# Two mixing layers rebuilt: one Block per layer, one ring of 68 weight slots, the delta rule in 84 steps between k-tiles

## What is computed

```python
def second_block(x, ...):
    for l in range(2):
        h = rms_norm_2(x, norm_w[l])
        p = h @ w_in[l]                       # 2048 x 6668
        qa, ka, va, za, ub, zb, qkv_c, b_c, a_c, zc = _split_cols(p)
        # branch A: 12 query heads of 64, 4 key heads, a causal window of 128, sinks
        oa = sliding_window_sink_attention(qa, ka, va, sinks[l]) * silu(za)
        # branch B: gated unit, 31-tap causal convolution on 512 channels, layer norm, 512 x 512
        ob = conformer_conv_module(ub, ...) * silu(zb)
        # branch C: 6 heads of 128, gated delta rule in chunks of 64 tokens
        oc = gated_deltanet(qkv_c, b_c, a_c, c_conv_w[l], c_a_log[l], c_dt_bias[l])
        oc = rms_norm_2(oc, c_onorm_w[l]) * silu(zc)
        x = x + concatenate([oa, ob, oc]) @ w_out[l]

def gated_delta_rule_chunked(q, k, v, g, beta):
    lower = where(strict, k*beta @ k.T * decay, 0)
    u, w = triangular_solve(lower + eye, [v*beta, k*beta*exp(gc)])
    for each chunk of 64:                     # four chunks
        v_new = u_i - w_i @ S                 # S is 0 before the first chunk
        o_i = (q_i * exp(g_i)) @ S + intra_i @ v_new
        S = S * exp(g_last) + (k_i * exp(g_last - g_i)).T @ v_new
```

## Time and profile before

| | |
|---|---|
| median of 3 runs | 2265.16 us (2264.9 to 2267.46) |
| the profiled execution's own time | 2267.13 us |
| its span | 2264.9 us |
| PE busy | 2066.9 us (91%) |
| DVE busy | 1328.0 us (59%) |
| ACT busy | 1083.8 us (48%) |
| HBM read | 321.78 MB |

### The profile page before, as it was taken

One profiled execution on the slowest core, in us unless ns is written; L12 is line 12 of the kernel. 1 busy time (PEld: TensorE's weight loads), 2 busy tenths in 40 slices (PEclk: granted clock), 3 DMA queues, 4 the chain that ended last, 5 costly groups with the idle time before them and its releaser, 6 DMA issues. The chain is left out here.

```text
span 2264.9 us, 32432 instructions
## 1 busy us (share of the span) xinstructions
PE 2066.9 (91%) x13116; PEld 1858.4 (82%) x13116; DVE 1328.0 (59%) x1900; ACT 1083.8 (48%) x1379; POOL 20.9 (1%) x22
## 2 busy tenths in 40 slices
PE   5999999999999999959798997779799789996979
PEld 5999889998888888859688996778698689985967
DVE  4887745554444465446647675854457375767633
ACT  5777645554333333356633466323456333663132
POOL 0001000000000000000000000000000000000000
PEclk9999999999999999979889898899899798998989
DMA  5455454444555556534244342006443243430043
GB/s 192 168 190 183 172 186 149 150 156 173 190 188 193 191 176 239 186 118 149 75 159 175 109 179 91 1 1 242 149 174 112 96 172 125 171 130 18 1 171 127
DMA packets 52403, 329.94 MB, mean 146 GB/s; under 512 B 7472, under 2 KB 9904, under 8 KB 14384
## 3 DMA queue, kind: packets, MB, share of 16 engines
q1 hardware_dynamic: 52272, 328.09, 40.3%
HBM read 321.78 MB, written 6.29 MB: 145 GB/s over the span
## 5 line engine op out<-in xcount | busy, mean ns | idle before, releaser
L350 DVE TENSOR_TENSOR w_lo<-w_raw,w_hi 128x2048 fp32r<-128x2048 f32 x184 | 425.8, 2315 | 392.4 <-ACT w_hi L343 392.3
L343 ACT ACTIVATE w_hi<-w_raw 128x2048 fp32r<-128x2048 f32 x184 | 352.3, 1918 | 404.6 <-PE z L377 304.9
L222 PE MATMUL z<-xn_hi,w_hi 128*128 128x256 f32 x1600 | 469.5, 293 | 33.8 <-DVEq L177 17.4
L222 PE MATMUL z<-xn_hi,w_lo 128*128 128x256 f32 x1600 | 458.8, 287 | 0.0
L222 PE MATMUL z<-xn_lo,w_hi 128*128 128x256 f32 x1600 | 458.2, 286 | 0.0
L194 DVE TENSOR_TENSOR w_lo<-w_raw,w_hi 128x2048 fp32r<-128x2048 f32 x104 | 238.4, 2292 | 195.6 <-ACT w_hi L190 195.5
L222 PEld LDWEIGHTS z<-xn_hi,w_hi 128*128 128x128 f32 x1600 | 310.0, 194 | 43.2 <-DVEq L177 19.4
L190 ACT ACTIVATE w_hi<-w_raw 128x2048 fp32r<-128x2048 f32 x104 | 199.1, 1914 | 277.6 <-PE z L222 260.8
L222 PEld LDWEIGHTS z<-xn_lo,w_hi 128*128 128x128 f32 x1600 | 310.6, 194 | 4.4 <-issue 4.3
L222 PEld LDWEIGHTS z<-xn_hi,w_lo 128*128 128x128 f32 x1600 | 309.0, 193 | 0.0
L377 PE MATMUL z<-w_hi,xn_hi 128*128 128x512 f32 x576 | 230.1, 399 | 0.0
(11 more groups left out here) (469 smaller groups left out, 3043.0 us busy)
## 6 DMA issues: line engine op xcount, KB each, us to landing
w_raw<-in_w_dram SPq DMA_DIRECT2D x288, 1024.0 KB, 4.8
gate_w<-in_lru_w_dram SPq DMA_DIRECT2D x8, 512.0 KB, 5.6
x_state<-state_dram SPq DMA_DIRECT2D x2, 2048.0 KB, 7.9
x_first<-in_x_dram SPq DMA_DIRECT2D x4, 512.0 KB, 7.7
x_t<-in_x_dram SPq DMA_DIRECT2D x1, 2048.0 KB, 11.7
state_dram<-x_t SPq DMA_DIRECT2D x2, 1024.0 KB, 3.9
din_pw<-in_pw_dram SPq DMA_DIRECT2D x2, 1024.0 KB, 5.5
state_dram<-x_state SPq DMA_DIRECT2D x8, 256.0 KB, 3.9
```

What stands on the lines that cost most here:

```text
L222: ins = pe.matmul(out, a, b, start=first and n == 0, stop=last and n == 2)
L343: act.activation(self.k.w_hi[:, n % SLOTS], self.k.w_raw[:, m % RAW], ACT.Copy).then_inc(self.s.rounded, 1)
L350: dve.tensor_tensor(self.k.w_lo[:, n % SLOTS], self.k.w_raw[:, m % RAW], self.k.w_hi[:, n % SLOTS].bitcast(F32), ALU.subtract).then_inc(se ...
```

## The change

`Stream` and the five phases are gone; `layer_block` is one Block per layer with one `Ring` of 68 slots in a new order: 8 for the gated unit, 2 + 2 for keys and values, 6 queries, 6 `za`, 18 for the heads of branch C (q, k, v in turn), 4 `zb`, 6 `zc`, 16 for `w_out`.

- The attention of unit `h` runs during the three slots of head `h`. Of the four 128 x 128 blocks of a head's scores, the one that the mask fills wholly (first queries, last keys) is no longer computed: scores, mask, softmax, transposes and the mix work on 384 columns and not 512.
- The transposes of the layer's input move from the end of the phase before to the first slot of the layer, two between k-tiles, as the first block has it at its own start.
- The narrow product is turned: the 12 columns are the weights, the tokens move (48 matmuls of 256 columns, line `narrow`), with a transpose behind it.
- Of the four taps of branch C's convolution ACT does the last (a copy with a scale), DVE three.
- The delta rule is cut into 28 batches x 3 groups = 84 steps, PE issuing one between two k-tiles in 14 of the 16 k-tiles of each of the six `zc` slots; DVE and ACT empty them in the same order (`evacuate`) behind the rounding and residual of that slot. The mask of a level is applied when its product leaves PSUM, so `BT` and its multiplication are gone. For the first chunk the products with the empty state are left out, and the copy takes the place of the multiply-add; after the last chunk no state is computed.
- In the last stage ACT takes the root of each group by itself: Ln, Exp, Ln, Exp, Ln, Exp.
- The layer's input is loaded in the middle of the ring, when slot 51 is done.

The diff, without the five phases and `Stream`, which are removed whole; its pieces are, in order, the ring, SP's loads, ACT's roots, two pieces of DVE's program, and PE's (the sum over branch B, one stage of a level, the `zc` slots, the token slots):

```diff
+    with phase(nc, f"layer{layer}", LAYER_SEMS) as s:
+        ring = Ring(k, s, SLOTS_1 + layer * SLOTS_2, SLOTS, SLOTS_2 + (SLOTS if more else 0))
...
+                for n in range(8, SLOTS_2 + 2 * SLOTS):
+                    ring.load(sp, n)
+                    if n == SLOT_OUT2 + 3:
+                        sp.wait_ge(s.used, SLOT_OUT2)
+                        sp.dma_start(x_t[:], t["state"]).then_inc(s.xin, 16)
...
+                ring.round(act, SLOT_OUT2 + 4)
+                for gr in groups:
+                    act.wait_ge(s.osum, gr.n + 1)
+                    act.activation(gr.XT, bank4(gr.b0), ACT.Ln, bias=k.eps[:], scale=1.0 / C_DIM).then_inc(s.orstd, 1)
+                    act.wait_ge(s.orstd, 2 * gr.n + 1)
+                    act.activation(gr.XT, gr.XT, ACT.Exp, scale=-0.5).then_inc(s.orstd, 1)
...
+                    if h == 1:
+                        taps(59, 3)
+                        branch_centre()
...
+                for n in range(SLOT_ZC, SLOT_OUT2):
+                    ring.residual(dve, n + 3)
...
+                    window(n)
...
+                    if n == 29:
+                        pe.wait_ge(s.taps, 2 * 2 * TAPS_B)
+                        pe.wait_ge(s.std, 2)
+                        branch_sum(acc).then_inc(s.bsummed, 1)
...
+                    elif b < 15 and stage == 1:
+                        pe.wait_ge(s.ucopied, 3 * (level - 1) + g + 1)
...
+                        for u in range(4):
+                            ins = pe.matmul(part4(gr.b1, u), gr.XT[:, u], gr.A[:, u], start=True, stop=True)
+                        ins.then_inc(s.xx, 1)
...
+                for n in range(SLOT_ZC, SLOT_OUT2):
+                    first_tick = TICKS * (n - SLOT_ZC)
+                    def between(kk):
+                        if kk < TICKS:
+                            step((first_tick + kk) // G, (first_tick + kk) % G)
+                    pe.wait_ge(s.emptied, n - 9)
+                    ring.features(pe, n, tile(bank_of(n)), k.xn_hi, k.xn_lo, between)
...
+                for c in range(4):
...
+                    for w in range(4):
+                        if c == 0 and w == 1:
+                            for g in range(G):
+                                sum_outputs(g)
+                        if c == 0 and w >= 2:
+                            pe.wait_ge(s.olo, 1 if w == 2 else 3)
+                        ring.tokens(pe, SLOT_OUT2 + 4 * c + w, w, pair(c), k.y_hi, k.y_lo)
```

More of the change, by code:

```diff
@@ L158, in _ @@
                     pe.sem_clear(sem)
[L161 to L218, removed]
-                    w_hi, w_lo = s_hi[:, kk, P * m:P * m + P], s_lo[:, kk, P * m:P * m + P]
-                    pairs = ((w_hi, hi[:, row]), (w_hi, lo[:, row]), (w_lo, hi[:, row]))
-                for n, (a, b) in enumerate(pairs):
-                    ins = pe.matmul(out, a, b, start=first and n == 0, stop=last and n == 2)
-        ins.then_inc(self.s.used, 1)
-    def done(self, i, s):
-        return SLOTS + 4 * i + s + 1
@@ L2433, in out_phase_2 @@
[L2433 to L2458 removed]
+                ring.load(sp, 4)
@@ new lines, in root @@
+                def root(bank, out, sem, before):
+                    act.activation(out, both(bank), ACT.Ln, bias=k.eps[:], scale=1.0 / HEAD_DIM_2).then_inc(sem, 1)
+                    act.wait_ge(sem, before + 1)
+                    act.activation(out, out, ACT.Exp, scale=-0.5).then_inc(sem, 1)
+                ring.round(act, SLOT_KV + 4)
+                key_in(0)
+                ring.round(act, SLOT_KV + 5)
+                key_in(1)
+                ring.round(act, SLOT_KV + 6)
+                act.wait_ge(s.kturned, 2)
@@ L2477, in square @@
+                for gr in groups:
+                    act.wait_ge(s.osteps, 2 * gr.n + 2)
+                    at = 10 + 2 * gr.n
+                    act.activation(k.y_hi[:, at:at + 2], by_head(gr.X), ACT.Copy).then_inc(s.orounded, 1)
+                ring.round(act, SLOT_OUT2 + 5)
+                ring.round(act, SLOT_OUT2 + 6)
                 def square(c):
@@ new lines, in _ @@
+                taps(40, 1)
+                ring.residual(dve, SLOT_ZA + 6)
+                taps(41, 4)
+                glink = chain(dve, s.gchain)
+                dve.wait_ge(s.zturned, 1)
+                for b in range(2):
+                    glink(lambda: dve.tensor_tensor(g_x[:, b], z[3][:, 16 * b + H:16 * b + 2 * H], rows[:, 1], ALU.add))
+                glink(lambda: dve.tensor_scalar(g_0[:], g_x[:], -1.0, None, ALU.mult))
+                glink(lambda: dve.tensor_tensor(g_0[:], g_0[:], g_x[:], ALU.min))
@@ new lines, in _ @@
+                pe.wait_ge(s.opened, 3)
+                for b in range(2):
+                    ring.features(pe, SLOT_KV + b, tile(b), k.xn_hi, k.xn_lo)
+                pe.wait_ge(s.opened, 4)
+                ring.halves(pe, SLOT_KV + 2, 0, (tile(2), tile(3)), k.xn_hi, k.xn_lo)
+                pe.wait_ge(s.turn_in, 16)
+                pe.wait_ge(s.kcopied, 2)
+                pe.wait_ge(s.emptied, 2)
+                pe.matmul(aux[0][:, 0:2 * T], turn[:], q_raw[1][:], start=True, stop=True).then_inc(s.kturned, 1)
```

2135 lines of the change are left out of this document (1011 added, 1124 removed).

## The result

The changed kernel takes **2158.06 us** (median of 4 runs, 2155.96 to 2162.24) against 2266.06 of the kernel before, measured beside it (4 runs, 2264.9 to 2267.46): 0.9525 of it, 95% interval 0.9513 to 0.9537, faster. The forecast was 2157, the range 2075 to 2235. The profiled execution is the slowest of the four, 2162.24 with a span of 2160.5, so its parts add up to 3.5 us more than the forecast's span.

The account below looks back on a forecast made before the run. PE was taken to bound the kernel: 517 us of PE's work and 59 of waits make a layer of 576. Start 986.3 + 576 + seam 14 + 576 + end 4.6 gives 2157 us, range 2075 to 2235.

Parts of the forecast that it names:

- PE's work: PE's own work in one layer at full clock, slots, fp32 inserts and delta steps included: 515 us.
- its price for the masked block: Leaving out a quarter of attention's scores, mixes and transposes was to save PE 4.3 us.
- The head slots: Slots 24 to 41: PE was to wait 20 us in a layer for late DVE and ACT.
- its own 92%: In slots 24 to 41, DVE and ACT each have 117 us of work against PE's 128, in strict order.
- The `zc` slots: Slots 46 to 51, with the delta steps between k-tiles: PE was to wait 17 us in a layer.
- every step pays its round trip: Rival, 5%: PE waits for emptying and two hand-overs at each of 168 delta steps, giving 2323 us.
- The output norm: PE's third token slot waits 12.4 us for `y_lo`, behind slot 56's load, a rounding and the roots.
- 4.8 past the end of slot 52: Slot 56's load, behind the 2 MB of `x_t`, was to land 4.8 us after slot 52 ends.
- The six table loads: In the output norm, ACT loads a table for each Ln and Exp in turn: 7.7 us on PE's wait.
- three waits, 2 each: Clock term: three waits a layer are longer than 3.49 us and cost 2 us each, 6 in all.
- the prediction's own sign of being wrong: The prediction is wrong if the clock is under 0.9 in a `zc` slot without a long wait.
- The end stays: From the last matmul to the kernel's end: 4.6 us, as in the kernel before.

Follow-up runs that it names:

- e3: Changed kernel with PE's sum over branch B behind slot 30 in place of slot 29: 2152.81 us, ratio 0.9505.
- e8: Changed kernel with PE again doing the masked attention block's products and transpose, into columns nobody reads: 2160.29 us, ratio 0.9537.
- e5: Changed kernel with delta steps between k-tiles only where PE had to wait, the others in rows behind slots 50 and 51: 2101.96 us, ratio 0.9276.
- e11: Kernel with e5 and e6 together, one of two copies of flipped scores moved from ACT to DVE: 2088.66 us, against 2087.9 without it.
- e4: Changed kernel with all 84 delta steps in one row behind slot 51, same Block and ring: 2143.91 us, ratio 0.9464.
- e2: Changed kernel with the 2 MB load of x_t issued behind the load of slot 56, not ahead: 2156.74 us, ratio 0.9521.
- e1: Changed kernel with three Ln together, then three Exp, in the output norm, so two table loads for six: 2150.63 us, ratio 0.9497.
- e6: Changed kernel with the roots grouped as in e1 and put ahead of ACT's rounding of slot 56: 2143.3 us, ratio 0.9458.
- e10: Changed kernel with the edits of e5, e6 and e3 together: 2081.88 us, ratio 0.9189.

## Why the prediction was right, and where not

**The sum and its parts.** 576 against 577.7 for the layer is in part luck. The waits came 14 lower and the clock 13 higher. Some 4.7 us of both are one thing on two sides, since a low clock ahead of a wait shortens it by as much (e3: 1.6 + 1.4 + 1.7); that the rest evened out was luck.

**PE's work** held: 515 against 517.4, although its price for the masked block, 4.3, was too low (about 7.5 by e8). For the steps, 130.4 less 34.5 for slots, 12.1 of waits and some 6.8 for the clock leaves 77.0; the forecast was 77, of which 4 were for going to and fro between streamed and fp32 work. e5, which has 15 steps between k-tiles and not 84, needs 73.2, which agrees with that.

**The head slots**: 20 forecast, 12.8 measured. The 5.4 us for DVE's taps came as walked through the queues (5.5), at the place named; the lateness of heads 1 and 2 came as 0.4 and that of heads 4 and 5 as 7.0. What the step did not draw from its own 92% is e3, e8 and e11: PE is not the bound in these slots, and a microsecond taken from a wait or from PE's work is not a microsecond won. The forecast counts leaving out the masked block as 4.3 us won; e8 shows about 0.

**The `zc` slots**: 17 forecast, 12.1 measured, each wait where it was put. Slot 46 has 1.98 and 2.95 (6 forecast), slot 47 has 2.23 (3), the scaled copies 2.40 (4). The rounding and then the residual at each slot's start, about 1 a slot, came as 1.24 in slot 48 and 1.33 in slot 49, some 5 us into the slot, and as nothing in slot 51. DVE's timeline shows the cause:

```profile
1377.82 2.29 DVE L253 TENSOR_TENSOR w_lo<-w_raw,w_hi 128x2048 fp32r<-128x2048 f32 x1 [2.38 <-ACT w_hi L246]
1380.03 0.68 DVE L2037 TENSOR_TENSOR unit<-aux,levels 128x512 f32<-128x512 f32 x1
...
1397.50 2.29 DVE L253 TENSOR_TENSOR w_lo<-w_raw,w_hi 128x2048 fp32r<-128x2048 f32 x1 [2.38 <-ACT w_hi L246]
```

DVE stands for 2.38 us before ACT's rounding, which itself waits for PE's last matmul of the slot before, then takes 2.29 for the residual, and only then empties the next step, on which PE waits until 1380.76. e5 has none of these waits; there the levels stand in a row with no rounding or residual between. The rival that every step pays its round trip is out: in the rows of e4 and e5 the levels run without a wait.

**The output norm**: 12.4 forecast, 9.47 and 8.37 measured. The term "4.8 past the end of slot 52" for the transfer is the one that failed: it cost 1.5 and 0.4 (e2). The rounding has to wait for the end of slot 52 in any case, and that slot began 2.5 us late and ran in part at a clock of 0.50, so that more of the 2 MB passed under it. The six table loads hold (e1, e6). For that order of Ln and Exp, the Trainium skill's ScalarE: Activation LUTs, section on table sets, has one load; the trace after does not agree either, with a load of 1.28 before each of the six. The Trainium skill's ScalarE: Activation LUTs, section What ACT_TABLE_LOAD costs, makes up the about 2.7 us that the prediction names of a load of about 1283 ns and a drain of about 1380 ns. The trace agrees with the load, 1.28, and shows no such drain: a load starts 0.02 us behind the operation before it (1471.60 to 1471.62), and its activation follows at once.

**The clock**: 6 for "three waits, 2 each" was the worst term, 18 measured. In this execution every wait of 1.98 us and more has a stretch at 0.50 with it, nine of them in the layer and not three, each costing 1.7 to 3 beyond the wait. This is also why the forecast's error in the waits did not show: shorter waits than forecast, more of them dear. Slot 46, with no wait over 3, had a mean clock of 0.87, which comes close to the prediction's own sign of being wrong, under 0.9 in a `zc` slot without a long wait.

**Not foreseen**: 2.53 at the first token slot, which needs the bank of slot 51. ACT empties it behind the rounding of slot 55, and both can start only when slot 51 is done.

**Seams**: start 987.1 (986.3 forecast), 13.7 (14, though its four terms add up to 13.3), end 7.3 (4.6). "The end stays" was wrong: the kernel before cleared 3 semaphores on PE there, the changed one clears 26, and PE is at it until 2160.2. The prediction charged more clearing at both starts and not here.

**What was missed altogether**: that the 84 steps between k-tiles are worse than the same steps in a row. The earlier trace rows showed it, sets 0.89 apart without a gap when nothing else was queued on DVE. The prediction used those rows for the price only, and not to ask what the placing itself brings. e4 and DVE's rows above show what that is.

## What to carry over

Put work of a dependent chain between streamed tiles only where the chain to another engine is longer than the rest of its own row; where three groups in rotation already hide it, a row of its own is faster, as the engine that empties it then has nothing else queued. Where two engines hand work to a third in strict order and all are near full, test by adding work to one before taking any away: if the time stays, that engine is not the bound. In an order written by hand, look for the operation that waits for nothing the next one needs (here a rounding ahead of the roots), and move it behind.

## What was not expected of the hardware

- A Block change that clears no semaphores left PE idle for 0.47 us in a running stream; 26 semaphores cleared by PE took 3.0 us.
- In the changed kernel the granted clock fell to 0.50 around or behind each wait of 1.98 us and more in an otherwise full stream, and stayed at 1.00 around waits of 1.24 and 1.33. But the same waits differ between executions: in layer 0 of e3 it stayed at 1.00 around those of 1.98, 2.23, 2.34 and 2.53, in layer 0 of e6 around the one of 2.52 for the root. Behind the wait of 2.20 for `y_lo` it stayed up in e6 and fell in layer 0 of e10. The four executions of the changed kernel stand in the order of their mean clocks, 0.973, 0.972, 0.971 and 0.969 for 2155.96, 2156.82, 2159.3 and 2162.24 us, so this may be why one kernel's times differ by some us.
- In e6 the table load ahead of an activation that has to wait is made before the wait, not after: the load of 1.28 stands at 1458.79, its activation at 1465.76.
